# Delta rule: the first 512 columns of z move in between the second pair's last phases

## What is computed

```python
def gated_delta_chunked(q, k, v, g, beta, s0):        # per head, chunk after chunk
    def step(S, inp):
        ...
        sol = lax.linalg.triangular_solve(a, rhs, left_side=True, lower=True, unit_diagonal=True)
        u, w = sol[..., :dv], sol[..., dv:]
        v_new = u - jnp.einsum('bhcd,bhde->bhce', w, S)
        ...
        S = (S * jnp.exp(g_last)[..., None] + jnp.einsum(..., v_new))
        return S, o

def deltanet_mixer(h_ctx, h_lat, w_in, ...):
    def prep(h):
        proj = h @ w_in
        ...
        z = proj[..., DN_CONV_W:DN_CONV_W + DN_VAL_W].reshape(B, T, DN_V_HEADS, DN_HEAD_DIM)
    def bidir(...):                                   # forward and backward in time
        return o_f + fl(o_b), s_f, s_b
    def out(o, z, dtype):
        o = rmsnorm(o, norm_g) * jax.nn.silu(z.astype(jnp.float32))
        return o.reshape(B, T, DN_VAL_W).astype(dtype) @ w_out
```

## Time and profile before

| | |
|---|---|
| median of 3 runs | 4298.86 us (4298.03 to 4300.78) |
| the profiled execution, its own time | 4287.95 us |
| its span | 4286.2 us |
| PE busy | 3650.8 us, 85% of the span |
| DVE busy | 2514.1 us, 59% |
| ACT, POOL busy | 966.8 us (23%), 1219.4 us (28%) |
| granted TensorE clock, mean | 0.966 of full |

### The profile page before, as it was taken

One profiled execution on the slowest core, in us unless ns is written; L12 is line 12 of the kernel. 1 busy time (PEld: TensorE's weight loads), 2 busy tenths in 40 slices (PEclk: granted clock), 3 DMA queues, 4 the chain that ended last, 5 costly groups with the idle time before them and its releaser, 6 DMA issues.

```text
span 4286.2 us, 59878 instructions
## 1 busy us (share of the span) xinstructions
PE 3650.8 (85%) x23128; PEld 1996.2 (47%) x23128; DVE 2514.1 (59%) x5831; ACT 966.8 (23%) x2602; POOL 1219.4 (28%) x1257
## 2 busy tenths in 40 slices
PE   7988899888899977776777789887777889899999
PEld 3467544675444432222232236443222368555774
DVE  3466435564566777776777655667776348535341
ACT  2333113331222222222222213222222121010100
POOL 1054000440134444444444400344444010015000
PEclk9999999899999999999999999999999999999999
DMA  8200244001599999999999933999999334330443
GB/s 291 83 4 4 89 158 158 4 4 50 201 384 404 410 419 420 418 415 412 411 413 416 413 123 121 412 416 418 412 414 415 134 93 138 123 103 20 143 146 127
DMA packets 270115, 1043.68 MB, mean 244 GB/s; under 512 B 19931, under 2 KB 104166, under 8 KB 171530
## 3 DMA queue, kind: packets, MB, share of 16 engines
q0 software_dynamic: 115184, 815.62, 46.7%
q1 hardware_dynamic: 154650, 224.23, 15.5%
HBM read 1038.64 MB, written 1.13 MB: 243 GB/s over the span
## 4 chain that ended last, share of the span: by engine, by line
PE 52%; DMA 25%; DVE 12%; ACT 4%; issue 4%; POOL 3%; SPq 0%; DVEq 0%; POOLq 0%; ACTq 0%
DMA arena<-in_peer_uv,arena 25%; PE psum L262 13%; PE psum L1858 12%; PE psum L772 5%; PE psum L300 5%; PE psum L1816 4%; PE psum L816 3%; DVE arena L1993 2%; PE psum L213 2%; PE psum L1162 1%; POOL arena L1951 1%; PE psum L508 1%; ACT arena L1893 1%; PE psum L1173 1%; POOL arena L3055 1%
## 5 line engine op out<-in xcount | busy, mean ns | idle before, releaser
L1858 PE MATMUL psum<-arena 128*128 128x512 f32 x3072 | 1458.9, 620 | 394.1 <-ACT arena L1893 389.3
L1993 DVE SCALAR_TENSOR_TENSOR arena<-arena 128x1024 bf16<-128x1024 f32 x768 | 941.0, 1225 | 523.6 <-DMA arena<-in_peer_uv,arena 492.1
L1951 POOL DMA_INDIRECT arena<-in_peer_uv,arena x768 | 855.4, 1114 | 1184.8 <-PE psum L1858 1055.2
L1858 PEld LDWEIGHTS psum<-arena 128*128 128x128 f32 x3072 | 573.8, 195 | 1227.8 <-ACT arena L1893 634.6
L262 PE MATMUL psum<-ring,arena 128*128 128x512 f32 (+1 forms) x1344 | 576.4, 590 | 24.6 <-DVE arena L2872 9.1
L262 PEld LDWEIGHTS psum<-ring,arena 128*128 128x128 f32 x1344 | 254.2, 192 | 340.3 <-issue 315.1
L1886 ACT ACTIVATE arena<-arena 128x2 f32<-128x2 f32 x384 | 78.2, 204 | 1242.7 <-DVE arena L1993 1242.7
L1893 ACT ACTIVATE arena<-consts,arena 128x128 f32<-128x128 f32 x768 | 268.4, 394 | 224.0 <-DVE arena L2005 221.5
L300 PE MATMUL psum<-arena,ring 128*128 128x256 f32 x1408 | 309.6, 381 | 9.8 <-DVE arena L2867 7.7
L300 PEld LDWEIGHTS psum<-arena,ring 128*128 128x128 f32 x1408 | 267.0, 191 | 50.4 <-issue 6.4
L772 PE MATMUL psum<-arena,ring 128*128 128x512 f32 x512 | 229.0, 600 | 1.6 <-issue 1.6
(11 more groups left out here) (412 smaller groups left out, 3894.9 us busy)
## 6 DMA issues: line engine op xcount, KB each, us to landing
arena<-in_ada_w SPq DMA_DIRECT2D x48, 1024.0 KB, 7.1
ring<-in_ffn_w_up SPq DMA_DIRECT2D x44, 1024.0 KB, 5.0
ring<-in_dn_w_in SPq DMA_DIRECT2D x24, 1024.0 KB, 5.6
ring<-in_peer_w_query SPq DMA_DIRECT2D x22, 1024.0 KB, 7.0
ring<-in_ffn_w_down SPq DMA_DIRECT2D x20, 1024.0 KB, 5.0
arena<-in_peer_uv,arena POOLq DMA_INDIRECT x768, 12.8
ring<-in_ev_w_in SPq DMA_DIRECT2D x10, 1024.0 KB, 5.1
ring<-in_dn_w_out SPq DMA_DIRECT2D x8, 1024.0 KB, 4.8
```

The lines of the kernel that those rows point to most:

```text
L1858: m = e.matmul(k.banks[4 + t % 2 * 2 + nh], self.diag[g % self.ND], self.vsl[g % self.NS][:, nh * 512:(nh + 1) * 512], start=u % 8 == 0 an ...
L1951: e.indirect_dma_start(self.uv[g % self.NS], None, self.table(), bass.IndirectOffsetOnAxis(ap=self.eid[u % 6][:, s:s + 1], axis=0)).then_i ...
L1993: e.scalar_tensor_tensor(self.junk[g % 2], self.us[g % self.NS], 1.0, self.h[:, u // 8, :], MUL, MUL, accum_out=self.a[u % 2][:, s:s + 1]) ...
```

## The change

PE's program takes a third generator, `pe_z_first`, into the turns. It holds the 32 matmuls of z's first 512 columns, two to a piece, 16 pieces, and it is asked for a piece after each of the second pair's last 13 phases; what is left is written behind them, ahead of the meeting. Its first piece waits for DVE's last update of the state of both chains of the first pair (in whose banks it writes) and for the ring. `TokenProj.pe` then begins with the second block of columns. The other engines' programs do not change, in either half.

```diff
-    def pe(self, e):
+    def pe(self, e, first=0):
         ring, P, nb = self.st.k.ring, self.st.P, len(self.banks)
-        for n0, nw in self.cols():
+        for n0, nw in self.cols()[first:]:
             for k0, nk in self.rows():
...
-            self.in_turns(self.pe_chain, e, half)
+            self.in_turns(self.pe_chain, e, half, self.pe_z_first(e, half))
             self.meet(e, P, ("chain", half))
-            self.z[half].pe(e)
+            self.z[half].pe(e, 1)
...
-    def in_turns(self, program, e, half):
+    def in_turns(self, program, e, half, behind=()):
 
         first, second = (program(e, half, self.chains[a:a + 2]) for a in (0, 2))
+        behind = iter(behind)
         for n in range(4 * self.PHASES + self.LAG):
             if n < 4 * self.PHASES:
                 next(first)
             if n >= self.LAG:
                 next(second)
+            if n > 4 * self.PHASES:
+                next(behind, None)
+        for _ in behind:
+            pass
+
+    def pe_z_first(self, e, half):
+
+        ring, P, z = self.k.ring, self.P, self.z[half]
+        e.wait_ge(*self.V.at((half, 3, self.chains[0], "S")))
+        e.wait_ge(*self.V.at((half, 3, self.chains[1], "S")))
+        for k0 in (0, 4):
+            key = (self.name, z.name, 0, k0)
+            e.wait_ge(*ring.ready(key))
+            w = ring.buf(key).rearrange("p (k n) -> p k n", k=4)
+            for t in range(4):
+                for q in range(4):
+                    m = e.matmul(z.bank(t, 0), self.hT[:, k0 + q, t * 128:(t + 1) * 128], w[:, q, :], start=k0 + q == 0,
+                                 stop=k0 + q == 7)
+                    if q == 1:
+                        yield
+                m.then_inc(*P.up((z.name, t, 0) if k0 else None))
+                yield
+            ring.free(key, P)
```

## The result

| | before | changed |
|---|---|---|
| median (range) of 4 runs each | 4298.44 us (4296.43 to 4300.78) | 4273.16 us (4269.97 to 4276.11) |
| ratio, 95% interval | | 0.9941 (0.9924 to 0.9958) |
| the profiled execution, its own time | 4287.95 us | 4274.84 us |
| its span | 4286.2 us | 4273.0 us |

The change is faster by 25.3 us; the interval of the ratio makes that 18 to 33 us. The forecast was 20.0 us and a time of 4278.9 us in a range of 4274 to 4289. The direction and the mechanism held, but the measured time lies 0.8 us under the lower end of the range: **the prediction was wrong in its range**.

The account below looks back on a forecast made before the run. PE was taken to be waiting and slow in each last half step. Per half 10.2 + 27.6 + 0.8 + 0.2 + 29.4 = 68.2 us, gaining 20.0 us together: 4298.9 - 20.0 = 4278.9 us, range 4274 to 4289.

Parts of the forecast that it names:

- What bounds the kernel: Last half step: PE waits mostly for ACT's copies, 9.0 us of gaps in half 0, and partly runs at 1.2 GHz.
- Phases at full clock, 10.2 us: Second pair's own phases, X5 through S, summed at full clock: 10.2 us a half.
- Pieces, 27.6 us, and switches, 0.8 us: 32 moved z matmuls at unchanged price, 27.6 us; ten changes between blocks and whole array, 0.8 us (0 to 1.6).
- the row's 0.08: Cost in us per tiling switch, from profiled kS and qS work; 0.16, X6's wait for T5, was the upper end.
- The slow first piece: First z piece behind kS: if the half clock reached a little into it, at most its 1.72 us.
- The covered gaps: Inside the half step: every gap (1.46 us at most) is shorter than a 1.72 us piece, so all are covered.
- The meeting and DVE's path, 0.2 + 29.4 us: Meeting costs 0.2 us; from there to turning O, DVE's 29.4 us is the bound by 0.4 us over PE's 29.0.
- The sign given for it: Profile after: PE's last gap before turning O would be 1.6 to 2.0 us, released by DVE.
- Sum, 68.2 us: First piece to turning O: 68.2 us a half against 78.4 and 78.0, gaining 10.2 and 9.8 us.
- So I let it move up rigidly: Output weights, next half and gathers behind each half were taken to shift earlier by the full gain.
- The slower rival: z pieces run at the half clock: 27.6 us lost per half, 4354 us for both; chance 0.06.
- some 2 to 3 us by which the stages behind may not move rigidly: Last contribution to the range's width of 4274 to 4289 us, for the stages behind the stretches.

Follow-up runs that it names:

- one block: Changed kernel with the 32 z matmuls in one block ahead of the meeting, nothing in the turns: 4295.22 us, ratio 0.9991 to before.
- the throwaway matmuls: Kernel before plus one overwritten z matmul in the gaps ahead of Y5, T5 and Y6 of each last half step: 4286.66 us, ratio 0.9977 to before.
- the spare matmuls: Changed kernel plus 12 overwritten z matmuls behind each half's meeting: 4292.32 us, ratio 0.9991 to before.
- the early mark: Changed kernel with PE's meeting mark ahead of the eight trailing z matmuls, so DVE starts earlier: 4274.83 us, ratio 0.9946 to before.

## Why the prediction was right or wrong

**What bounds the kernel** was read right, but for two small things: the 0.16 us ahead of X6 is a wait for PE's own T5 and not for ACT, and between vn at half clock and o at full clock lies qS with 2.36 us, where the clock changed. Without the pieces in the turns only 3.7 us stay (one block), so it is the gaps, and the low clock of the phases among them, that the change takes away. The forecast did not claim how the gain splits; the throwaway matmuls show 3.5 us a half for the clock in the phases.

**Phases at full clock, 10.2 us:** 9.7 in the changed kernel. X5 0.39, Y5 0.38, T5, X6 and Y6 0.61 each, as taken. But a group of eight instructions between two pieces is spaced by 0.89 us (984.93 to 985.82) where 0.965 was taken from back-to-back groups, and qS by 1.73 against 1.84.

**Pieces, 27.6 us, and switches, 0.8 us:** a piece ahead of a whole-array phase takes 1.72 us (985.82 to 987.54), one ahead of a 32x32 or 64x64 phase 1.91 (973.24 to 975.15). Ten switches cost about 1.0 us together. The Trainium skill, "TensorEngine Tiling (Array Packing)", Key Properties, says that a change of tiling mode drains the array. The trace agrees with it in one direction: 0.19 us in front of a blocked phase. That this is the drain is not shown, and on the way back to the whole array nothing is seen. So the mean is 0.1 a switch, and the row's 0.08 was nearer than the 0.16. The slow first piece, priced at up to 1.7 us, cost 0.1 to 0.6 us in half 0 and nothing in half 1.

**The covered gaps** were covered, all of them: no release by ACT is seen in the turns.

**The meeting and DVE's path, 0.2 + 29.4 us:** 29.2 to 29.3 from the end of the trailing matmuls. DVE did become the bound, by 0.15 us. The products ran in 5.8 us, not the 6.05 taken (0.65 + 3 x 1.57 + 0.69). The sign given for it, a last gap of PE of 1.6 to 2.0 us, did not come: it is 1.41 to 1.46 us, since the lead of DVE's path is so small.

**Sum, 68.2 us:** 67.5 to 68.1 in six halves, 67.7 in the mean. In the first profile the terms were 0.6 us a half too dear, 1.2 us in all.

**"So I let it move up rigidly"** held within what can be seen: with the spare matmuls 18.0 of 20.7 us arrived at the end, and the time behind half 1 is 3232.5 us before and 3234.4 after in the first two profiles. If anything the stages behind took longer, not shorter.

**The slower rival** had its mechanism in the kernel, but on the other side. The granted clock does not fall under the pieces; the pieces are what keeps it up, and what falls now and then is the clock under z in the kernel before. The forecast took before's stretch from one execution, in which that did not happen.

**The step that failed** is the width, and in it the last term: "some 2 to 3 us by which the stages behind may not move rigidly", with the carrying of a difference of two traces to a median of a few runs. Everything outside the two stretches was put at nothing in the sum, and its scatter was judged from three runs within 2.8 us. The runs showed this in its place:

- The two stretches gained 21.8 us, not 20.0. So 1.8 us are mis-sized terms: before's two stretches together are 0.75 us longer in the mean of its five profiles than in the one, and the changed kernel's sum was 0.5 us a half too dear (10.2 against 9.7 for the phases, 29.6 against 29.2 from the meeting on, 0.8 against 1.0 for the switches the other way).
- The other 3.5 of the 25.3 us lie in no stretch. Runs of before spread over 14 us, and the start of X5 in half 0 lay between 445.9 and 455.2 us into the span in profiles of before, with no edit ahead of it. A median of four drawn from such runs is off by over 2 us in three draws of ten, an estimate from the 63 timed runs of before. All runs on record, 67 of before with a mean of 4297.8 us and 10 of the changed kernel with 4274.1, give 23.6 us, within about 2. So some 1.7 of the 3.5 us were the draw of the runs.
- About 2 us are left beyond the stretches, at the edge of what these runs can tell. Every version in the table above has such an excess, and no trace shows its place. Its cause stays open.

That the time fell 0.8 us outside the range was partly bad luck: with a gain of 23.6 us it would have lain just inside. The width was too narrow all the same.

No version was shown to beat the changed kernel: one matmul to a piece is 24.9 us below before and the early mark 24.1, between the 22.6 and 25.3 of the changed kernel's own two measurements.

## What to carry to other kernels

When an engine waits several times for 1.5 us in a short dependent sequence, independent work from behind it, cut in pieces a little longer than the gaps, is worth the gaps plus what the low TensorE clock costs in the phases between them. Here that was 10.9 us in each last half step: 3.5 for the clock, shown by the throwaway matmuls, and 7.4 for the rest, by subtraction. Cost such a stretch by adding up PE's work at full clock, and compare that sum with the traced length: the two agreed here within 1 us in 68. Take the scatter for the range from more than three runs, or from the spread of a marker in several traces. More than one profile is also needed to see what happens only in some executions.

## What was not expected of the hardware

- The gaps can cost more than themselves and the phases among them. In 3 of 13 traced halves that end as before does (ten of before, one with the move in half 0 alone, two with the throwaway matmuls), z, dense and without a wait, took 56.58, 56.87 and 58.18 us in place of 55.17. The granted clock over its first 5, 5 and 9 us was 0.71, 0.67 and 0.67. PE had been busy for 2.25 of 4 us in the S phases ahead of the last of them, and for 2.15 of 4 us in a half where the clock then stayed up.
- A single 0.86 us matmul in three gaps of 1.45 us kept the clock at 1.00 from X5 to S in both halves, though 0.4 us of each gap stayed. The same kernel without them ran those phases at 0.50.
- Eight 128x128 instructions are spaced by 0.89 us between long matmuls and by 0.965 among their like.
